# Expert rows gathered with their inverse root as a column, first two lists before the ranking, the other lists behind experts

## The reference, cut to what matters

```
h   = rmsnorm(x2, g_ffn_norm)
grp = argmax(h @ w_rg + b_rg)                 # one of 4 groups of 8 experts
top 2 experts of that group; gates = softmax over groups and over the two
for every expert e:  y = (silu(xb @ w_g[e]) * (xb @ w_u[e])) @ w_d[e]    # xb: the rows of h that chose e
out = x2 + sum of the two gated y;   final rmsnorm
```

## Time and profile before

| | us |
|---|---|
| median of 3 runs | 2269.15 |
| lowest, highest | 2263.95, 2270.84 |
| profiled execution | 2271.61 |
| its span | 2269.8 |
| PE busy | 1896.4 (84%) |
| DVE busy | 670.1 (30%) |
| ACT busy | 259.5 (11%) |
| POOL busy | 272.5 (12%) |

### The profile page before, as it was taken

The page is one execution under the profiler, slowest core; times in us unless marked ns, Lnnn a source line. Parts: engine busy times, 40 slices in busy tenths (PEclk is TensorE's granted clock), DMA queues, the critical chain, the costliest instruction groups (busy, mean ns, idle before and its releaser), DMA issues.

```text
span 2269.8 us, 22167 instructions
## 1 busy us (share of the span) xinstructions
PE 1896.4 (84%) x8836; PEld 1191.1 (52%) x8836; DVE 670.1 (30%) x1243; ACT 259.5 (11%) x471; POOL 272.5 (12%) x187
## 2 busy tenths in 40 slices
PE   7798995898569989999399989897988978777870
PEld 6687884787338868888354343342433323222320
DVE  6700999432963321000550111111011101001106
ACT  3002110002231120111300000000000000000002
POOL 0731322101920000000000100000000000000000
PEclk9899997999779999999679999899999989988985
DMA  5153122234912412432629999999999999999957
GB/s 213 56 149 93 67 74 92 101 139 140 5 60 81 160 38 111 166 113 75 242 82 407 387 401 411 391 412 411 405 395 403 387 402 414 407 407 397 409 205 298
DMA packets 91141, 545.10 MB, mean 240 GB/s; under 512 B 27984, under 2 KB 40784, under 8 KB 44400
## 3 DMA queue, kind: packets, MB, share of 16 engines
q1 hardware_dynamic: 70512, 520.50, 60.6%
q0 software_dynamic: 5888, 17.05, 2.2%
q10 hardware_dynamic: 14656, 6.33, 1.3%
HBM read 523.07 MB, written 37.26 MB: 247 GB/s over the span
## 4 chain that ended last, share of the span: by engine, by line
PE 41%; DMA 24%; DVE 7%; issue 2%; ACT 1%; SPq 1%; DVEq 0%; POOLq 0%
DMA arena<-w_up_in 23%; PE psum L566 13%; PE psum L882 8%; PE psum L847 6%; PE psum L840 3%; PE psum L843 3%; PE psum L698 2%; PE psum L823 1%; DVE arena L1406 1%; PE psum L692 1%; DMA arena<-y_rows 1%; SPq L483 1%; DVE arena L1400 1%; DVE arena L1398 1%; DVE arena L1608 1%
## 5 line engine op out<-in xcount | busy, mean ns | idle before, releaser
L566 PE MATMUL psum<-arena 128*128 128x260 f32 x3328 | 755.0, 390 | 38.9 <-ACT arena L928 12.5
L566 PEld LDWEIGHTS psum<-arena 128*128 128x128 f32 x3328 | 646.0, 195 | 143.9 <-issue 29.0
L847 PE MATMUL psum<-arena 128*64 128x512 f32 x832 | 404.8, 645 | 110.7 <-DMA arena<-w_up_in 110.7
L849 PE MATMUL psum<-arena 128*64 128x512 f32 x832 | 405.4, 646 | 0.0
L847 PEld LDWEIGHTS psum<-arena 128*64 128x64 f32 x832 | 120.1, 149 | 377.6 <-issue 377.6
L882 PE MATMUL psum<-arena 128*64 128x512 f32 (+1 forms) x1024 | 277.1, 608 | 17.7 <-ACT arena L1086 17.0
L882 PEld LDWEIGHTS psum<-arena 128*64 128x64 f32 (+1 forms) x1024 | 96.2, 150 | 176.0 <-issue 153.6
L1673 DVE TENSOR_TENSOR arena<-arena,psum 64x512 f32<-64x512 f32 x26 | 18.0, 691 | 492.6 <-ACT arena L1083 492.6
L1200 POOL DMA_INDIRECT y_rows<-arena x32 | 30.0, 937 | 998.5 <-DVE arena L1682 967.1
L1682 DVE COPY arena<-psum 64x512 f32<-64x512 f32 (+1 forms) x64 | 43.5, 687 | 282.4 <-PE psum L882 281.6
L849 PEld LDWEIGHTS psum<-arena 128*64 128x64 f32 x832 | 120.1, 149 | 0.0
(11 more groups left out here) (311 smaller groups left out, 1480.0 us busy)
## 6 DMA issues: line engine op xcount, KB each, us to landing
arena<-w_gate_in SPq DMA_DIRECT2D x64, 2048.0 KB, 38.3
arena<-w_up_in SPq DMA_DIRECT2D x64, 2048.0 KB, 42.7
arena<-w_down_in SPq DMA_DIRECT2D x64, 2048.0 KB, 41.8
arena<-w_in_in SPq DMA_DIRECT2D x32, 1024.0 KB, 4.8
arena<-w_out_in SPq DMA_DIRECT2D x16, 1024.0 KB, 4.8
arena<-k_cache_in SPq DMA_DIRECT2D x8, 1024.0 KB, 6.7
arena<-v_cache_in SPq DMA_DIRECT2D x8, 1024.0 KB, 4.8
arena<-y_rows SPq DMA_DIRECT2D x4, 2048.0 KB, 19.4
```

The source lines that it names most:

```text
L566: last = mm(pair(n)[:, h, :], w(kk), rhs(kk)[:, HALF * h:HALF * (h + 1)], start=(kk == 0), stop=(kk == kn - 1 and stop))
L847: lastg = mm(ps[0:SLIM, 2, :], xt[:, 8 * hf + kk, :], wg[:, kk, :], start=(hf == 0 and kk == 0), stop=(hf == 1 and kk == 7))
L849: lastu = mm(ps[SLIM:P, 2, :], xt[:, 8 * hf + kk, :], wu[:, kk, :], start=(hf == 0 and kk == 0), stop=(hf == 1 and kk == 7))
```

## The change

The normalised rows are no longer made. `x2_rows` gets rows of 2064 floats: 2048 of x2, and 16 copies of the row's inverse root. ACT, not SP, stores x2, on its own DMA queue after each group's last square, and then the five column tiles. The gather takes x2 rows with their column; ACT scales the identity by that column (`dx`), and PE turns the rows by a matrix product with this diagonal instead of a transpose with the identity. POOL's clearing and gathers wait for x2 stores and column stores.

The lists are made in 28 groups. Group 0 (experts 0 and 1, whose ranks are fixed) comes right after the position sums, before the ranking; groups 1 and 2 (experts 6 to 14 and 2 to 5) behind expert 0's gate and up; the other 25, two at a time, behind the `down` of experts 0 to 12 (`LATE` is 13). The rest of the routing (room, blocks, overflow) is computed after the first turned rows. Routing scratch and early selections lie in slot 9's region alone, indices behind it, so slot 8 is released by `s_lg` and slot 9 by `s_free`. SP loads 4 to 6 as soon as the projection ends, 7 after the x2 stores, then 8, 10, 11, 9, 12 and so on.

```diff
-GROUPS = [(0, 6, CAP), (6, 15, SLIM), (15, 24, SLIM), (24, 32, SLIM), (32, 38, CAP), (38, 44, CAP), (44, 48, CAP)]
+EARLY = 3
+GROUPS = ([(0, 2, CAP), (6, 15, SLIM), (2, 6, CAP)] + [(b, min(b + 2, NE), SLIM) for b in range(15, NE, 2)]
+          + [(b, b + 1, CAP) for b in range(NE, NBLK)])
+ROWW = DM + 16
...
+        rt = Cols(at["A"] + HALFW)
+        scratch_at = rt.at
+        early_sel = [view(scratch_at, 640), yrow[:, 0:1440], view(scratch_at, 1280)]
...
+        LATE = (len(GROUPS) - EARLY + 1) // 2
... (SP)
             for n in range(2, 16):
-                if n % 4 == 3 and n > 4:
-                    store_x2(n // 4 - 1)
                 sp.wait_ge(s_op, n - 1)
...
-            store_x2(3)
 
             sp.wait_ge(s_op, 16)
             for n in range(4, 6):
                 load_next(n, 0)
             load_next(6, 1)
-            for i, n in enumerate(TOKS):
-                sp.wait_ge(s_hr, i + 1)
-                sp.dma_start(h_rows[P * i:P * i + n, :], x2_of[i][0:n]).then_inc(s_hst, 16)
...
-            sp.wait_ge(s_hst, 16 * 5)
+            sp.wait_ge(s_x2st, 16 * 8)
+            sp.wait_ge(s_rss, 20)
             load_next(7, 1)
-            sp.wait_ge(s_idx, len(GROUPS))
-            for n in range(8, 12):
+            sp.wait_ge(s_lg, 1)
+            load_next(8, 1)
+            for n in (10, 11):
                 load_next(n, 1)
+            sp.wait_ge(s_free, 1)
+            load_next(9, 1)
             sp.wait_ge(s_ord, 1)
... (PE)
-            def turn_rows(j, gathered, cap, turned):
+            def late_lists(i):
+
+                for g in range(EARLY + 2 * i, min(EARLY + 2 * i + 2, len(GROUPS))):
+                    lists(g, ps[:, 0, 8 * (g % 2):8 * (g % 2) + 8])
+
+            def turn_rows(j, diagonal, cap, turned):
 
-                pe.wait_ge(s_gat[j], gathered)
-                rows = xrow[j][0:cap, :].rearrange("p (m k) -> p k m", k=16)
+                pe.wait_ge(s_dx, diagonal)
+                rows = xrow[j][0:cap, 0:DM].rearrange("p (m k) -> p k m", k=16)
...
-                        last = pe.transpose(ps[:, g % 2, cap * m:cap * (m + 1)], rows[:, per * g + m, :],
-                                            ident[0:cap, 0:cap])
+                        last = mm(ps[:, g % 2, cap * m:cap * (m + 1)], rows[:, per * g + m, :],
+                                  dx[j][0:cap, 0:cap], start=True, stop=True)
...
-            for g in range(3):
-                lists(g)
-            turn_rows(0, 16, CAP, 0)
+            lists(0, ps[:, 4, :])
+            turn_rows(0, 1, CAP, 0)
             for i in range(NE):
                 slots, uses = slots_of(i)
                 gate_up(WIDE[i], slots, uses, TURNED[i + 1], i)
+                if i + 1 < NE:
+                    if 1 <= i <= LATE:
+                        pe.wait_ge(s_idx, min(EARLY + 2 * i, len(GROUPS)))
+                    turn_rows((i + 1) % 2, i + 2, CAP if WIDE[i + 1] else SLIM, TURNED[i + 1])
                 if i == 0:
-                    for g in range(3, len(GROUPS)):
-                        lists(g)
-                if i + 1 < NE:
-                    turn_rows((i + 1) % 2, 16 * ((i + 1) // 2 + 1), CAP if WIDE[i + 1] else SLIM, TURNED[i + 1])
+                    for g in range(1, EARLY):
+                        lists(g, ps[:, 4 + g, :])
                 turn_act(WIDE[i], i)
                 if i == 0:
-                    pe.wait_ge(s_idx, len(GROUPS))
+                    pe.wait_ge(s_idx, EARLY)
                 down(WIDE[i], slots, uses, i)
+                if i < LATE:
+                    if i + 1 < NE:
+                        pe.wait_ge(s_xte, TURNED[i + 2])
+                    late_lists(i)
... (ACT)
+                if i == 4:
+                    c = slice(512 * g, 512 * (g + 1))
+                    act.dma_start(x2_rows[0:SEQ, c].rearrange("(i p) n -> p i n", p=P), x2row[:, 0:4, c]
+                                  ).then_inc(s_x2st, 16)
+                    act.dma_start(x2_rows[SEQ:T, c], x2_of[4][0:NS, c]).then_inc(s_x2st, 16)
...
-            act.wait_ge(s_rrs, 2)
-            act.wait_ge(s_x2st, 16 * 8)
+            act.wait_ge(s_rsc, 1)
             for i, n in enumerate(TOKS):
-                A(x2_of[i][0:n], x2_of[i][0:n], ACT.Copy, scale=row_rstd[0:n, i:i + 1]).then_inc(s_hr, 1)
+                act.dma_start(x2_rows[P * i:P * i + n, DM:ROWW], rstd_cols[0:n, i, :]).then_inc(s_rst, 16)
...
+            def scale_rows(j, gathered, n, cap):
+                act.wait_ge(s_gat[j], gathered)
+                if type(n) is not int or n > 1:
+                    act.wait_ge(s_at, n - 1)
+                A(dx[j][0:cap, 0:cap], ident[0:cap, 0:cap], ACT.Copy, scale=xrow[j][0:cap, DM:DM + 1]).then_inc(s_dx, 1)
...
+            scale_rows(0, 16, 0, CAP)
             for i in range(NE):
+                if i + 1 < NE:
+                    scale_rows((i + 1) % 2, 16 * ((i + 1) // 2 + 1), i + 1, CAP if WIDE[i + 1] else SLIM)
                 expert(i, WIDE[i])
... (POOL)
-            pool.wait_ge(s_hst, 16 * 5)
+            pool.wait_ge(s_x2st, 16 * 8)
+            pool.wait_ge(s_rst, 16 * 5)
... (DVE)
+            dve.tensor_copy(rstd_cols, row_rstd.unsqueeze(2).to_broadcast([P, 5, 16])).then_inc(s_rsc, 1)
...
             dve.wait_ge(s_pos, 1)
+            link(stt(posblk[:, :, 0:2], ps[:, 1, 0:160].rearrange("p (t e) -> p t e", t=5)[:, :, 0:2], 1.0,
+                     m16[:, :, 0:2], ALU.add, ALU.mult))
+            select(0)
...
+            lists(0, ps[:, 4, :])
+            dve.wait_ge(s_x2st, 16 * 8)
...
+            dve.wait_ge(s_gt, 16)
+            rows_turned(CAP, 0)
             link(ts(room, place, float(NWIDE), float(CAP - SLIM), ALU.is_lt, ALU.mult))
...
             select(1)
-            select(2)
-            lists(1)
-            lists(2)
...
+            select(2)
+            for g in range(EARLY, EARLY + 2):
                 select(g)
...
+                if i == 0:
+                    for g in range(1, EARLY):
+                        lists(g, ps[:, 4 + g, :])
+                    dve.sem_inc(s_free, 1)
                 rows_out(i, WIDE[i])
+                if i < LATE:
+                    dve.wait_ge(s_lst, min(EARLY + 2 * i + 2, len(GROUPS)))
+                for g in range(EARLY + 2 * i, min(EARLY + 2 * i + 2, len(GROUPS))):
+                    lists(g, ps[:, 0, 8 * (g % 2):8 * (g % 2) + 8])
+                for g in range(EARLY + 2 * i + 2, min(EARLY + 2 * i + 4, len(GROUPS))):
+                    select(g)
```

More of the change, by code:

```diff
@@ L170, in build @@
         ro_at = at["cos"]
[L172 to L176, removed]
+        xrow = [view(ms + ROWW * j, ROWW) for j in range(2)]
+        xtr = view(ms + 2 * ROWW, 16 * CAP)
+        actv = view(ms + 2 * ROWW + 2048, 512)
+        actt = view(ms + 2 * ROWW + 2560, 4 * CAP)
+        yrow_at = ms + 2 * ROWW + 3072
+        yrow = view(yrow_at, DM)
         ring = [ring0 + HALFW * j for j in (4, 5, 6, 7, 1, 2, 3, 0)] + [at["A"], at["A"] + HALFW]
@@ L294, in build @@
         assert late.at <= at["cos"]
[L296 to L300, removed]
+        none = stat[:, 44:62]
+        rstd_cols = region("lr", 80).rearrange("p (t c) -> p t c", t=5)
+        late_sel = [view(ro_at + 30, 320), region("lr", 320)]
+        dx = [view(ro_at + 350 + P * j, P) for j in range(2)]
+        rt = Cols(at["A"] + HALFW)
+        scratch_at = rt.at
+        order_t = [yrow[:, NE * NE * j:NE * NE * (j + 1)].rearrange("p (a b) -> p a b", a=NE) for j in range(2)]
+        early_sel = [view(scratch_at, 640), yrow[:, 0:1440], view(scratch_at, 1280)]
         def sel16(g):
@@ L469, in _ @@
                 load_w(n, t["w_out"][n])
[L471 to L477, removed]
             def load_half(slot, j, e):
@@ L1191, in gather @@
                 pool.indirect_dma_start(
-                    out=xrow[j][0:cap, :], out_offset=None, in_=h_rows,
+                    out=xrow[j][0:cap, :], out_offset=None, in_=x2_rows,
                     in_offset=bass.IndirectOffsetOnAxis(ap=index, axis=0),
@@ L1529, in _, with two, select, lists @@
             link(ts(tok1, tok, 1.0, None, ALU.add))
+            def two(ap):
+                return ap.rearrange("p (t b) -> p t b", t=5)
+            tt(two(first_a), hot1[:, :, 0:2], full(id_[:, 0:5], 2), ALU.mult)
+            link(tt(two(first_b), hot2[:, :, 0:2], full(id_[:, 5:10], 2), ALU.mult))
+            tt(rv16[:, :, 0:2, 0:1], two(first_a).unsqueeze(3), two(first_b).unsqueeze(3), ALU.add)
+            link(dve.tensor_copy(rv16[:, :, 0:2, 1:2], full(tok1, 2).unsqueeze(3)))
+            def select(g):
+                b0, b1, cap = GROUPS[g]
+                if g >= EARLY + 2:
+                    dve.wait_ge(s_lst, g - 1)
+                tt(sel16(g), iota_s[:, 0:cap].unsqueeze(1).unsqueeze(1).to_broadcast([P, 5, b1 - b0, cap]),
+                   posblk[:, :, b0:b1].unsqueeze(3).to_broadcast([P, 5, b1 - b0, cap]),
+                   ALU.is_equal).then_inc(s_sel, 1)
+            def lists(g, out):
+                b0, b1, cap = GROUPS[g]
```

(34 more changed lines are left out.)

80 lines of the change are left out of this document (25 added, 55 removed).

## The result

The changed kernel takes 2302.22 us in the median (four runs, 2300.63 to 2303.62), the kernel before 2266.55 beside it (2263.17 to 2270.84): a ratio of 1.0156, with a 95% interval from 1.0134 to 1.0178. It is slower by 36 us where 2251 had been forecast. The profiled executions, on which all that follows is read, take 2302.13 and 2271.61, 30.5 apart.

What follows compares the result with a forecast made beforehand. The prediction took the stream of 192 expert-weight halves to bound the kernel; starting it 20.8 us earlier, less 1.8 for holes, gives 19 off 2271.6, 2252.6, by the median 2250, stated as 2251, range 2243 to 2266.

Steps and rivals of the forecast that it cites:

- Step 4: Turning rows on PE as diagonal products: 0.114 us a record, +1.7 us a slim expert, ends 0 and +5.9.
- Rival B: Turning rows, experts 2 to 18: PE becomes the bound, from 0.19 us a record; 2300 us, chance 0.07.
- step 6: Weight stream: half 22 moves from 1237.7 instead of 1258.5, 20.8 us earlier, no hole; experts average 31.0 against 32.4.
- Step 1: Storing x2 rows from ACT: issues cost +1.0 us, last store lands at 1107 (1103.7 to 1111), columns at 1109.
- Step 2: First list in the routing: ready at 1112, where the first full selection started at 1126.04 before.
- Step 3: First gather and scaled diagonal: PE starts turning rows at 1121.5, 19 us earlier; ends 1118 and 1136.
- rival A: Stores or first gather: rows stay late beside the halves; gain only 5 to 12 us, 2261, chance 0.13.
- Step 5: Expert 0 to expert 1: 24 us of DVE work mostly covered, down 14.00; expert 1 starts at 1181.9, not 1201.65.
- rival C: Lists 1 and 2 late, slot 9 shut: the front moves, the stream doesn't; 2268 us, chance 0.08.

Runs made afterwards that it cites:

- e2: The kernel before, with PE turning rows by products with the identity in place of its transposes: 2312.57 us (one run).
- e3: The changed kernel, its turning products reading 128 neighbouring columns instead of every sixteenth (output not the layer's): 2241.64 us (one run).
- e4: Rows scaled on ACT and turned with transposes, as the changed kernel otherwise, but every transpose issued twice: 2245.10 us (one run).
- e1: The changed kernel, with ACT scaling the gathered rows in place and PE turning them with transposes again: 2248.28 us, ratio 0.9918.
- e9: e1, with halves 4 to 8 issued only after the gathers of experts 0 and 1: 2238.77 us in the median of five, one of them 3647.66.
- e5: e1, with halves 4 to 6 issued only when x2 is stored: 2245.63 us, ratio 0.9892.
- e6: e1, with halves 8, 10 and 11 held back until the routing's scratch is free, as half 9 is: 2256.72 us, ratio 0.9950.

## Why the prediction was wrong

**Step 4, the price of a turning record, failed.** The prediction saw that a product is two records and bounded it between a record half as long as a transpose's and one of 0.248 us, then took 0.114 from the router's row "since the router's row is also fp32, with 128 columns loaded, at full clock". The runs show 0.225 in the change and in e2, 0.120 in e3 with contiguous columns. So the row chosen differed in the one thing that decides, the stride of 16 elements between the columns loaded. The prediction had seen the stride and set it aside, because the transposes read with the same stride at 0.125. That row was of another operation: for a transpose the stride cost nothing to be seen, for an fp32 product it nearly doubled the record. A slim expert's turn cost 7.2 instead of 3.65.

The step had a second part missing: it held the clock at 1.00 outside expert 0. The clock was 0.50 behind the turn shown above, and the mean slim down was 1.6 us dearer; in e3 and e4, where it falls too, this was hidden.

**Rival B is what happened**, at 2300 by its working and 2302 in the runs. It put the border at 0.19 us a record and the four experts at 35.3; they took 35.8. Its 49 us over 17 experts were 48.3 over 16. Its 20 us of lead came in other places than it said: only 3.8 by expert 2, the rest in the 12 slim experts and the tail, where PE at 30.7 an expert outran the old stream's 31.5. So near a number is in part luck: B had every record at 0.248, the price of a transpose at a granted clock of 0.50, which is 5.9 us more an expert; the runs have 0.225, mostly at a clock of 1.00, which is 5.2 more for the turn and 1.6 for down. The prediction gave it a chance of 0.07, though its step 6 said that the cover was 1.4 us in 32.4. With its extra spread evenly over its own ends, 0 to 5.9, the border of 4.2 would have left B (5.9 - 4.2)/5.9 = 0.29: the row of the router had been given more weight than a row of another access pattern can bear.

The Trainium skill (Perfetto Trace Analysis, section Transposes) says to use the transpose for a logical transposition and not a plain product; the runs agree for rows read with this stride, with 2248.28 in e1 against 2302.22, and it was a rule that spoke against this change; in e3, with neighbouring columns, the plain product cost no time to be seen (2241.64 in one run).

**Step 1** was near. The two store issues on ACT ran beside the root, not ahead of it, as the timeline of ACT after shows:

```profile
1097.54 0.37 ACTq L1073 DMA_DIRECT2D x_rows<-arena  x1
...
1098.49 0.30 ACT L1077 ACTIVATE arena<-arena 128x5 f32<-128x5 f32 x1 [0.24 <-DVE arena L1507]
```

1098.49 against 1098.36: +0 of the two ends, not +1.0. The x2 store took its late end, 1111 instead of the middle, 1107, and POOL clears at 1112.20, 3 late. The prediction had argued from turns, packet by packet, that the store would not wait for all three halves. The DMA packets that the profile records show the turns, and why they did not help: from 1103 to 1108 us SP's queue and ACT's queue start 109 packets each, but a packet of a half is 16 KB and one of the store 2 KB, so the store gets a ninth of the bytes until the halves are through.

**Step 2** holds: the list was ready at 1110.66 (1112 forecast). **Step 3**: from the gather's issue at 1116.79 to PE at 1124.95 are 8.2 us (7.9 forecast). With step 1's 3 us this makes the first turn 3.4 late, short of rival A's 1130. That was not the floor: e9 brings it to 28.1 us after the projection from 34.5. The gather is slow beside the halves for the reason of the store: in e5, from 1116 to 1124 us, 231 packets of the gathers, 216 of them of 4 bytes, alternate with 233 of the halves, 201 of them of 16 KB. The Trainium skill (DMA: Bandwidth & Descriptors, section Queues, rings and completion order) has an engine take turns between the rings that have work; these counts agree, and so do the gather's 4.6 to 11.9 us, the more the halves beside it.

**Step 5**: the turn for expert 0 took 7.25 (7.9), its gate and up 27.7 (29.5), and DVE's moved work ended at 1156.6 against PE's 1160.70, so the cover held and rival C is out. Behind it the next turn was 6.88 instead of 4.0, for step 4's reason. Down was 16.56 instead of 14.0, and that is an error of step 5 alone: e1, with transposes, has 16.82 there. The prediction took 14.00 "as PE hardly idles before it"; PE hardly idles, and yet the granted clock is 0.50 at the start of this down, in the kernel after as in e1 (its down, then the windows of both):

```profile
1162.13 16.82 PE psum L884 x32
```
```profile
1171.30:1175.30 4.00, 4.00 (x5) 1.80 (x6) 0.00 (x0) 0.00 (x0) 0.06 (x1) 0.50 0.95 352
```
```profile
1162.10:1166.10 4.00, 3.97 (x5) 1.85 (x6) 0.00 (x0) 0.00 (x0) 0.37 (x1) 0.50 0.93 332
```

Expert 1 started at 1188.56 instead of 1181.9; 2.9 of these 6.7 us are the turn's and 2.6 are down's.

**Step 6** was right where nothing of step 4 enters: half 9 left at 1170.31 (1167 forecast, 1175 the border of C), 10 at 1147.00 (1146.0). The rest of the step, a stream without holes, failed with step 4. e1, with that taken out, lands at 2248.28 by a forecast of 2251. The sum held better than its first steps: e1's first turn comes 35.9 us after the projection, where the forecast has 1121.5 - 1090.5 = 31.0.

## What to carry to other kernels

Price an operation by a row that reads its operands as the new one will, with the same stride and operation, and where there is none, let the far end of the bound decide whenever the slack is smaller than the distance to it. Scaling that rides on a product is free only while that product is no dearer than what it replaces; an engine that idles, ACT here, scaled for nothing. A small transfer that everything waits for goes ahead of a bulk stream that has room behind it: e9 gained about 10 us over e1 from two waits that hold 10 MB back, while holding the store's rivals alone (e5) or the gather's at the price of a late half 8 (e6) did not.

## What the runs showed of the hardware

- An fp32 product whose stationary columns lie 16 elements apart: 0.225 us a record, 0.120 with neighbouring columns (e3), both 64 rows by 128 columns. The loads of these columns take 308 and 193 ns. A transpose over the same stride: 0.124 (e1).
- The granted clock falls while PE is busy by the profile: from 1.00 to 0.50 within 6.7 us of turning (after); it is 0.57 behind 3.45 us of turning (e3), 0.60 in e4, still 1.00 behind 2.0 us (before). At the start of expert 0's down, behind 65 small list products, it is 0.50 after and in e1 alike.
- Two DMA queues with work take turns by packets, not by bytes: 109 packets of 16 KB beside 109 of 2 KB in 5 us (after), 233 beside 231 in 8 us (e5). The last x2 store let POOL's clearing start 12.6 us after the projection without halves beside it and 21.7 with them (e5, e1).
- Six halves passed in 30.7 us in the last 12 experts after, where PE sets the pace and the medians from issue to landing are 15.3 to 18.9 us; before, with a deep queue, six took 31.5 there. What makes the difference was not tried.
